# A hybrid decoder step on one Trainium2 core: the MLP and the gate by one level of Strassen's scheme

## The reference

```
def _channel_and_ple(h, mix, p_l, w_out, g_ffn, w_up, w_down, w_ple, w_ple_norm, w_ple_gate):
    h = h + mix @ w_out                                            # w_out 2048 x 2048
    u = _rmsnorm(h, g_ffn)
    h = h + jnp.square(jax.nn.relu(u @ w_up)) @ w_down             # 2048 x 8192, 8192 x 2048
    e = _rmsnorm(p_l @ w_ple, w_ple_norm) * jax.nn.sigmoid(h @ w_ple_gate)   # 256 x 2048, 2048 x 2048
    return h + e
```

## Time and profile before

| | |
|---|---|
| time, three runs | 2848.83, 2850.85, 2850.91 us; median 2850.85 |
| span of the profiled execution | 2847.1 us |
| PE busy over the span | 95% |
| DVE, ACT, POOL busy over the span | 46%, 27%, 20% |
| moved from HBM, written | 377.71 MB, 15.58 MB |

### The profile page before, as it was taken

The page is one execution under the profiler, slowest core; times in us unless marked ns, Lnnn a source line. Parts: engine busy times, 40 slices in busy tenths (PEclk is TensorE's granted clock), DMA queues, the critical chain, the costliest instruction groups (busy, mean ns, idle before and its releaser), DMA issues.

```text
span 2847.1 us, 50247 instructions
## 1 busy us (share of the span) xinstructions
PE 2696.2 (95%) x21759; PEld 2573.3 (90%) x21759; DVE 1320.5 (46%) x1501; ACT 774.8 (27%) x967; POOL 582.7 (20%) x290
## 2 busy tenths in 40 slices
PE   7999999967767999999999999999999999999998
PEld 7999999923346999999999999999999999999998
DVE  4277877628468224333333433333333333346433
ACT  3111111137643223222222222222222222223222
POOL 0098999300036011100000000000000000002322
PEclk9999999988876999999999999999999999999999
DMA  4388888489813222332333233333333333322233
GB/s 132 107 277 269 279 299 285 138 344 353 311 55 121 86 76 81 104 100 94 97 103 98 90 104 97 98 96 104 102 99 97 96 98 98 103 90 89 90 97 112
DMA packets 294896, 396.43 MB, mean 139 GB/s; under 512 B 14773, under 2 KB 256051, under 8 KB 292982
## 3 DMA queue, kind: packets, MB, share of 16 engines
q1 hardware_dynamic: 271688, 380.23, 40.4%
q10 hardware_dynamic: 22990, 13.01, 1.6%
HBM read 377.71 MB, written 15.58 MB: 138 GB/s over the span
## 4 chain that ended last, share of the span: by engine, by line
PE 79%; DVE 6%; POOL 5%; DMA 4%; issue 2%; SPq 2%; ACT 2%; ACTq 0%; DVEq 0%; POOLq 0%
PE ps L1180 25%; PE ps L1182 25%; PE ps L1185 25%; POOL kpage L1029 4%; DMA kpage<-in_cache_k 2%; DMA vpage<-in_cache_v 2%; DVE wl L1672 1%; PE ps L1280 1%; PE ps L1560 1%; SPq L470 1%; POOL dl L1074 1%; DMA xs<-in_x_sample 0%; ACT wh L608 0%; DVE se L1829 0%; POOL bx L1082 0%
## 5 line engine op out<-in xcount | busy, mean ns | idle before, releaser
L1180 PE MATMUL ps<-uh,wh 128*128 128x260 f32 x4512 | 1184.9, 284 | 20.1 <-DVE wl L1672 14.1
L1182 PE MATMUL ps<-ul,wh 128*128 128x260 f32 x4512 | 1180.5, 283 | 0.0
L1672 DVE TENSOR_TENSOR wl<-raw,wh 128x1024 fp32r<-128x1024 f32 (+1 forms) x418 | 590.4, 1413 | 1242.9 <-ACT wh L608 1242.8
L608 ACT ACTIVATE wh<-raw 128x1024 fp32r<-128x1024 f32 (+1 forms) x418 | 440.6, 1055 | 1803.6 <-PE ps L1185 1755.3
L1185 PE MATMUL ps<-uh,wl 128*128 128x260 f32 x4512 | 907.6, 283 | 0.0
L1180 PEld LDWEIGHTS ps<-uh,wh 128*128 128x128 f32 x4512 | 853.1, 189 | 22.9 <-DVE wl L1672 11.8
L1182 PEld LDWEIGHTS ps<-ul,wh 128*128 128x128 f32 x4512 | 851.3, 189 | 0.0
L1185 PEld LDWEIGHTS ps<-uh,wl 128*128 128x128 f32 x4512 | 696.4, 189 | 0.0
L1180 PE MATMUL ps<-hh,wh 128*128 128x260 f32 x2048 | 536.1, 283 | 0.0
L1182 PE MATMUL ps<-hl,wh 128*128 128x260 f32 x2048 | 534.1, 282 | 0.0
L1185 PE MATMUL ps<-hh,wl 128*128 128x260 f32 x2048 | 410.7, 282 | 0.0
(11 more groups left out here) (340 smaller groups left out, 1502.6 us busy)
## 6 DMA issues: line engine op xcount, KB each, us to landing
kpage<-in_cache_k SPq DMA_DIRECT2D x128, 512.0 KB, 4.9
vpage<-in_cache_v SPq DMA_DIRECT2D x128, 512.0 KB, 6.1
raw<-in_w_up SPq DMA_DIRECT2D x128, 512.0 KB, 3.6
raw<-in_w_down SPq DMA_DIRECT2D x128, 512.0 KB, 3.4
raw<-in_w_in SPq DMA_DIRECT2D x88, 512.0 KB, 4.6
raw<-in_w_out SPq DMA_DIRECT2D x32, 512.0 KB, 3.5
raw<-in_w_ple_gate SPq DMA_DIRECT2D x32, 512.0 KB, 3.4
xt<-in_x_prompt SPq DMA_DIRECT2D x8, 1024.0 KB, 9.0
```

The costliest lines, as they stand in the source:

```text
L608: A(wh[:, c % 2, 0:elems], raw[:, c % 2, 0:elems], ACT.Copy).then_inc(hi_ready, 1)
L1180: mm(ps[:, bank + 2 * m + f, 0:HALF], h_, xh[:, f * HALF:(f + 1) * HALF], start=st, stop=False)
L1182: mm(ps[:, bank + 2 * m + f, 0:HALF], h_, xl[:, f * HALF:(f + 1) * HALF], start=False, stop=False)
L1672: tt(wl[:, c % 2, 0:elems], raw[:, c % 2, 0:elems], wh[:, c % 2, 0:elems].bitcast(F32), ALU.subtract).then_inc(lo_ready, 1)
```

## The change

Up, down and gate each are products of a weight matrix with 520 token columns. They are now done by one level of Strassen's scheme (in Winograd's form). The weights are cut in even and odd tiles of 128 rows and of 128 columns, the activations in even and odd tiles of rows and in two halves of 260 tokens. A **group** is 2048 weight rows by 256 columns, as four blocks (11, 12, 21, 22) of 8 tiles each. A group takes 7 products instead of 8; each product is 8 tiles by 260 tokens in 24 matrix instructions (16 with the weights' high part, 8 with the rest). There are 72 groups: 32 of up (g 0 to 31), 32 of down (g 32 to 63, four chunks of 2048 hidden rows by 8 column groups), 8 of gate (g 64 to 71).

- DVE makes four sums of weight blocks for each group (`sum_t1` to `sum_t4`) and the rest of seven block operands (`w_low`). ACT makes the seven high parts (`w_high`).
- Seven operands of activations (`ah`, `al`, places 0 to 8) serve a whole phase: all of up, one chunk of down, or all of gate. A change of phase, from up to down, between chunks of down and from down to gate, is called a turning here. For down the operands' sums are made on POOL (`hidden_sums`) and stored in DRAM (`o_scr`) after each up group, and loaded back as 7 operands of 1040 KB (`operand`) at the turnings. There their second halves' rests are POOL's, from the third operand on (`a_low_second`), the others DVE's (`a_low`).
- The results of a group are combined from four PSUM banks by ACT and DVE in pieces of 128 x 260 (`x_rd`, `ev`). Up's pieces go through relu and square on ACT. The norm's factor is squared and applied only once, to the finished sum of down, on POOL (`h_complete`).
- Down's partial results lie in DRAM (`d_scr`); in chunks 1 to 3 they are loaded, added to (`add_first`, `add_second` on POOL, the rest on DVE) and stored again.
- PLE stands ahead of up, and h and e are kept in DRAM (`h_scr`, `e_scr`).
- Weight blocks have 128 columns, so rows of 512 bytes.

```diff
+GU, GD, GG = 0, 32, 64
+GN = 72
+KP = 8
+
+
+        def w_block(g, odd_rows, odd_cols):
+
+            if g < GD:
+                w, row, col = d["w_up"][0], 0, 256 * g
+            elif g < GG:
+                w, row, col = d["w_down"][0], 2048 * ((g - GD) // 8), 256 * ((g - GD) % 8)
+            else:
+                w, row, col = d["w_ple_gate"][0], 0, 256 * (g - GG)
+            w = w[row:row + 2048].rearrange("(j e p) n -> e p j n", e=2, p=P)
+            return w[odd_rows][:, :, col + P * odd_cols:col + P * odd_cols + P]
+
...
+                    load_out(SL_OUT + 4 * g + j)
+                h_store(g - 1)
...
-            for i in range((CHUNKS - 2) // 2):
-                load_up(SL_MLP + 8, 1, 2, 32, i)
-                load_down(SL_MLP + 16, 0, 2, 32, i)
-                load_up(SL_MLP + 24, 2, 2, 32, i)
-                load_down(SL_MLP + 32, 1, 2, 32, i)
...
+                if g == 1:
+                    h_store(7)
+                    for m in range(2):
+                        sp.wait_ge(h_out[m], 16 * 4)
+                    sp.wait_ge(s_hg, KT)
+                    block22(0)
+                    block12(0)
+                    block11(0)
+                    block22(1)
+                if g >= 3:
+                    e_store(g - 3)
+            e_store(5)
+            e_store(6)
+            sp.wait_ge(lo_ready, SL_ALL + 2)
+            block21(0)
+            e_store(7)
+
...
+            for g in range(GN):
+                if GD + 8 <= g + 1 < GG:
+                    down_load(g + 1)
+                if g > GD and g <= GG - 8:
+                    down_store(g - 1)
+                last_up, c = g == GD - 1, (g - GD) // 8
+                turning = last_up or (g >= GD and g < GG - 8 and (g - GD) % 8 == 7)
+                if turning:
+                    operand(c + 1, 2)
+                if g + 1 < GN:
+                    block12(g + 1)
+                if 1 <= g <= GD:
+                    hidden_store(g - 1)
+                if turning:
+                    operand(c + 1, 3)
+                    operand(c + 1, 4)
+                if g + 1 < GN:
+                    block11(g + 1)
+                if turning:
+                    operand(c + 1, 5)
+                if g + 1 < GN:
+                    block21(g + 1)
+                if turning:
+                    operand(c + 1, 6)
+                if g + 2 < GN:
+                    block22(g + 2)
+                if g == 27 or (g >= GD and g < GG - 8 and (g - GD) % 8 == 3):
+                    operand(c + 1, 0)
+                    operand(c + 1, 1)
...
+            def w_high(w):
+                g, i = w // 7, w % 7
+                if w < 2:
+                    act.wait_ge(w_used, SL_PLE + 6 + w + 3)
+                else:
+                    act.wait_ge(wh_used, WH_USED0 + w - 1)
+                    act.wait_ge(w_lo, W_LO0 + w - 1)
+                if i == 0:
+                    act.wait_ge(b_in[b11(g)], B_IN0[b11(g)] + 16 * (g + 1))
...
+                A(wh3[:, w % 2], w_source(g, i), ACT.Copy).then_inc(w_hi, 1)
...
+            def relu_square(g, k, src):
+                chain(A(st[:, k], src, ACT.Relu))
+                A(st[:, k], st[:, k], ACT.Square).then_inc(o_sq, 1)
...
+                        if up:
+                            if g:
+                                act.wait_ge(o_out, 16 * g)
+                            else:
+                                act.wait_ge(w_used, SL_ALL + 2)
+                            chain(A(st[:, 0], bank(g, 0), ACT.Relu))
+                            act.sem_inc(a_free, 1)
+                            A(st[:, 0], st[:, 0], ACT.Square).then_inc(o_sq, 1)
...
+            def hidden_sums(g):
+                pool.wait_ge(o_sq, O_SQ0 + 4 * g + 3)
+                step(pool.tensor_tensor(st[:, 4], st[:, 7], st[:, 5], ALU.add))
+                step(pool.tensor_tensor(st[:, 3], st[:, 0], st[:, 7], ALU.subtract))
+                step(pool.tensor_tensor(st[:, 1], st[:, 4], st[:, 0], ALU.subtract))
+                pool.wait_ge(o_sq, O_SQ0 + 4 * g + 4)
+                pool.tensor_tensor(st[:, 6], st[:, 2], st[:, 1], ALU.subtract).then_inc(o_sum, 1)
+
...
+            def add_first(g):
+                q = g - GD
+                both = dt3[q % 3].rearrange("p m n -> p (m n)")[:, HALF:3 * HALF].rearrange("p (x n) -> p x n", x=2)
+                pool.wait_ge(d_in[q % 3], D_IN0[q % 3] + 16 * ((q - 8) // 3 + 1))
+                pool.wait_ge(ev, EV0 + 5 * g + 1)
+                pool.tensor_tensor(both, both, xsc[:, 1].unsqueeze(1).to_broadcast([P, 2, HALF]), ALU.add)\
+                    .then_inc(d_add, 1)
+
+            def add_second(g):
+                part = dt3[(g - GD) % 3][:, 1, HALF:T]
+                pool.wait_ge(ev, EV0 + 5 * g + 2)
+                pool.tensor_tensor(part, part, xsc[:, 2], ALU.add).then_inc(d_add, 1)
+
+            def a_low_second(phase, i):
+                n = place_of(phase, i)
+                pool.wait_ge(a_hi, A_HI0 + 2 * (7 * phase + i) + 2)
+                pool.tensor_tensor(al[n][:, 4:8], af[n][:, 4:8], ah[n][:, 4:8].bitcast(F32), ALU.subtract)\
+                    .then_inc(al_p, 1)
+
...
+            def h_complete(g):
+                dt_ = dt3[(g - GD) % 3]
+                pool.wait_ge(ev, EV0 + 5 * g + 5)
+                if g == GG - 8:
+                    pool.wait_ge(r_sq, R_SQ0 + 1)
+                    pool.wait_ge(hr_in, 32)
+                step(pool.tensor_tensor(dt_, dt_, rstd.unsqueeze(1).to_broadcast([P, 2, T]), ALU.mult))
+                h_ = hT[:, g - GG + 8]
+                pool.tensor_tensor(h_, h_, dt_, ALU.add).then_inc(h_fin, 1)
...
+            BANK_OF = (0, 1, 0, 2, 3, 2, 3)
+
+            def product(g, i, phase):
+                w, n = 7 * g + i, place_of(phase, i)
+                pe.wait_ge(w_hi, W_HI0 + w + 1)
+                out, fresh = bank(g, BANK_OF[i]), i in (0, 1, 3, 4)
+                for k in range(KP):
+                    if g == GG and k == 7:
+                        pe.wait_ge(q_lo7, Q_LO70 + (0, 1, 2, 4, 5, 3, 6)[i] + 1)
+                    mm(out, wh3[:, w % 2, k], ah[n][:, k], start=fresh and k == 0, stop=False,
+                       skip_group_check=True)
+                    last = mm(out, wh3[:, w % 2, k], al[n][:, k], start=False, stop=False,
+                       skip_group_check=True)
+                last.then_inc(wh_used, 1)
+                pe.wait_ge(w_lo, W_LO0 + w + 1)
+                for k in range(KP):
+                    last = mm(out, wl3[:, w % 2, k], ah[n][:, k], start=False, stop=k == KP - 1,
+                              skip_group_check=True)
+                last.then_inc(wl_used, 1)
...
+            for g in range(GN):
+                c, j = (g - GD) // 8, (g - GD) % 8
+                phase = 0 if g < GD else min(1 + c, 4)
...
+                for i in range(7):
+                    if g == GU:
+                        pe.wait_ge(al_a, AL_A0 + i + 1)
+                        pe.wait_ge(al_b, AL_B0 + i + 1)
+                    elif GD <= g < GG and j == 0:
+                        pe.wait_ge(al_a, AL_A0 + 7 * phase + i + 1)
...
+                    if i == 5:
+                        pe.wait_ge(ev, EV0 + 5 * g + 2)
...
+            def sum_t3(g):
+                dve.wait_ge(b_in[b22(g)], B_IN0[b22(g)] + 16 * (g // 2 + 1))
+                dve.wait_ge(b_in[b12(g)], B_IN0[b12(g)] + 16 * (g + 1))
+                if g:
+                    dve.wait_ge(t_sum, T_SUM0 + 4 * (g - 1) + 3)
+                    dve.wait_ge(w_lo, W_LO0 + 7 * (g - 1) + 4)
+                tt(rb[B_T], rb[b22(g)], rb[b12(g)], ALU.subtract).then_inc(t_sum, 1)
+
+            def sum_t1(g):
+                dve.wait_ge(b_in[b11(g)], B_IN0[b11(g)] + 16 * (g + 1))
+                dve.wait_ge(t_sum, T_SUM0 + 4 * g + 1)
+                tt(rb[b12(g)], rb[b12(g)], rb[b11(g)], ALU.subtract).then_inc(t_sum, 1)
+
+            def sum_t2(g):
+                dve.wait_ge(t_sum, T_SUM0 + 4 * g + 2)
+                dve.wait_ge(w_lo, W_LO0 + 7 * g + 1)
+                tt(rb[b11(g)], rb[b11(g)], rb[B_T], ALU.add).then_inc(t_sum, 1)
+
+            def sum_t4(g):
+                dve.wait_ge(t_sum, T_SUM0 + 4 * g + 3)
+                dve.wait_ge(w_lo, W_LO0 + 7 * g + 3)
+                tt(rb[B21], rb[B21], rb[b11(g)], ALU.subtract).then_inc(t_sum, 1)
+
+            def w_low(w):
+                dve.wait_ge(w_hi, W_HI0 + w + 1)
+                if w >= 2:
+                    dve.wait_ge(wl_used, WL_USED0 + w - 1)
+                tt(wl3[:, w % 2], w_source(w // 7, w % 7), wh3[:, w % 2].bitcast(F32), ALU.subtract).then_inc(w_lo, 1)
+
...
+            def gate_pair7():
+                dt_ = dt3[(GG - 1 - GD) % 3]
+                dve.wait_ge(ev, EV0 + 5 * (GG - 1) + 5)
+                dve.wait_ge(hr_in, 32)
+                link(tt(dt_, dt_, rstd.unsqueeze(1).to_broadcast([P, 2, T]), ALU.mult))
+                tt(hT[:, 7], hT[:, 7], dt_, ALU.add).then_inc(h_fin, 1)
...
+                    if i == 6:
```

(29 more changed lines are left out.)

909 lines of the change are left out of this document (595 added, 314 removed).

## The result

The changed kernel takes **3015.38 us** (median of 4 runs, 3009.14 to 3019.8) against 2850.88 us (2848.83 to 2852.13) for the kernel before: a ratio of 1.0579, 95% interval 1.0562 to 1.0596. It is 5.8% slower where 4.3% faster was forecast. The profiled run has a span of 3007.4 us, 160.3 more than before.

What follows compares the result with a forecast made beforehand. PE's instruction list was taken to bound MLP and gate: -209.9 us, plus 29, 4, 21, 3, 8 and 21 of waits, gives -123.9 against the span of 2847.1, hence 2723.2 and a median of 2727 us; range 2680 to 2790.

Steps and rivals of the forecast that it cites:

- What bounds, PE's spacing, PE's list: MLP and gate: PE's instruction list bounds, 0.1198 us each; 13824 instructions become 12096, -209.9 us.
- Hidden with 1 us to spare: 0: Transfers in a group: hidden store lands near 11.5, product 5's high part ready at 13.5, due at 14.4; adds 0.
- rival 2: Hidden store lands 2 or 3 us later, costing 1 or 2 us in each of 31 groups: 2758 to 2789; chance 0.12.
- State updates: +4: Up groups with a state update: POOL's extra 5.7 us covered on average over three groups; 8 x 0.5, +4 us.
- Turnings +21: Four phase changes: DVE's and POOL's added work exceeds PE's time; 4.5 us three times, 8 from up to down, +21.
- Covered on average: State updates in up: three groups' DVE and POOL work is 55.8 us of PE's 60.3.
- Last chunk +3: Last chunk of down: `h_complete` adds 2.44 + 1.92 us to seven groups; +3 us, at most 10.
- Start of the gate +21: Groups 63 and 64: PE waits for gate operands; group 64 takes 42 us instead of 20.1, +21, at least 11.
- Gate groups +8: Gate groups: multiplication by e, scaling and additions on DVE and POOL cost seven times about 1.1, +8 us, at most 14.
- PLE and group 0 +29: PLE and up's first group: late w_ple, operands and rests; up starts in effect at T+59 instead of 29.8, +29 us.
- Rival 3: POOL's work is added in full to DVE's, no overlap: +46 us, 2773 us; chance 0.17.
- Rivals 1 and 4: 1: DVE's and POOL's sums hide, 2667 us, chance 0.18. 4: 512-byte-row blocks land late at `sum_t3`, slower than before, 0.04.

Runs made afterwards that it cites:

- store_first: Changed kernel with SyncE issuing the store of the hidden rows ahead of block 12 of the next group instead of behind it; 2886.67 us, ratio 1.0143.
- repeats: Changed kernel with ScalarE's piece behind product 5's high part, plus that high part made 4 to 16 times more in six down groups; 2986.84 us.
- no_state: Changed kernel with ScalarE's piece behind product 5's high part, minus GpSimd's three instructions of each state update in up; 2918.84 us.
- no_pool_mlp: `all1` with all of GpSimd's work in up and down moved to VectorE; 2793.1 us.
- all1: `store_first` plus state updates over three groups, gate's U3 ahead of third sum, gate's operands on VectorE, h completed behind the additions; 2859.96 us, ratio 1.0044.
- no_pool_all: `no_pool_mlp` with the gate's sums of squares and multiplication of e also moved from GpSimd to VectorE; 2780.67 us, ratio 0.9762.
- no_pool_late: `no_pool_all` with the store of the hidden rows behind block 12 again, as in the changed kernel; 2935.73 us.

## Why the prediction was wrong

**What bounds, PE's spacing, PE's list: right.** 20.1 us a group wherever nothing waits (third window of the result), -209.9 us.

**"Hidden with 1 us to spare: 0": the step that failed.** It is rival 2's mechanism at more than its size. The order of the store alone is worth 129 us, of 288 between forecast and measurement, 114 of them in groups 1 to 30: 3.8 us a group where rival 2's worst case had 2. Two numbers were off, both the same way. SyncE starts block 12 8.4 us into the group and not 5.6 (7.9 in `store_first`, in a group without any wait): `sum_t4` is queued behind product 2's rest, and that waits for its high part. In down the 5.6 was right: there SyncE starts it 5.8 us into group 34, which begins at 2077.9.

```profile
2083.69 0.37 SPq L657 DMA_DIRECT2D rb<-in_w_down  x1
```

In up ScalarE has relu and square of the last piece of the group before ahead of that high part in its queue, and 5.6 us leaves no room for them: the high part comes 4.2 us into group 13 of `store_first` and 2.1 us into group 34. The store lands 7.6 us after its issue and not 5.5: I added 1.4 us for the block in front, and `store_first` shows 3.0. Even from its own figures the sum was optimistic. How 3.2 us for 512 KB and 75% more bytes make the landing near 11.5 is not said; in proportion the store takes 5.6 us, which with the start at 5.6 and the 1.4 makes a landing at 12.6 and a high part at 14.6, behind the 14.4 at which it is due. 8.8 + 7.6 is 16.4, plus 2.0 for relu, square and high part is 18.4 against a due time of 14.4; the trace has 3.5 us of wait, as product 5 would have begun at 14.9 and not at 14.4. An estimate with 1 us of slack over a chain of five terms was booked at nothing and given 0.12, which the working does not bear out.

**The missing term: the clock.** The sum priced a wait at its own length. The trace has 72 us of starts at 1.2 GHz behind waits, 40 of them in up; `repeats` shows the wait to be the cause. The windows of the kernel before had shown the clock below 1 only outside the stretches that I priced, and nothing in the working asked what a wait does to it.

**"State updates: +4": too small.** The 3.2 us and their clock come to about 6 us in each of 8 groups (47 in `store_first`); `no_state` takes 25 off. "Covered on average" was the error: PE asks for each product's parts in turn, with 1 or 2 us of slack, and the three instructions come together.

**Turnings +21: 63.** They are 24.0 in groups 31 and 32, where the store takes part, and 12.9, 13.4 and 13.0. Both lists were added, which was right, but GpSimd's rest of 1040 was taken at 1.92 us: it takes 2.43 with VectorE idle and up to 3.45 beside it, three in a row 10.11. The lower clock (14 us of the 63) was left out. With all of the work on VectorE (`no_pool_mlp`) the turnings in down still cost 8.5 to 8.8 each, so the sharing explains only about a third; what holds the rest no run separates.

**Last chunk +3: 27.7.** 10 of it is group 57, where POOL stands 16.9 us for hT from DRAM ahead of the additions, which I did not cost at all, and 6 group 63. Groups 58 to 62 have a wait of up to 1.5 us each, from GpSimd's completion of h; when VectorE does it, groups 59 to 62 take 20.2.

**Start of the gate +21: 39.4.** The list was walked in the right order, with about 2.8 us for each of GpSimd's six instructions; they took 4.0 to 5.9 and made VectorE's as long.

**Gate groups +8: 31.9.** Where the wait was to be I had not said. It is mostly U3's (19.2 us), behind a third sum that waits 1.65 us for its block and then takes 3.08 beside GpSimd's 2.40.

**PLE and group 0 +29: 34.5.** Nearly right: the second group started at T+84, predicted T+79. GpSimd's instructions of 2080 elements took 5.4 and 5.5 us, where 3.1 were put in, and VectorE's two rests beside them 11.2.

**The rule on SBUF.** The Trainium skill, "SBUF — State Buffer", "Who interferes with whom", has the second of the two blocked until the first finishes. The traces agree in every pair shown here: VectorE's rest of 1820 elements, 2.04 us without GpSimd, took 5.87 when it began 1.05 us after a GpSimd instruction of 5.01. Rival 3 took it as "POOL's work is added in full", +46 on top of the part that the forecast already held. In the runs taking the work off GpSimd is worth 79 us (`all1` to `no_pool_all`), with the operands of the gate 96. When both engines had a queue they alternated, and both lists, not one, grew to the sum.

**Rivals 1 and 4.** Nothing hid (1). Blocks with 512-byte rows did land late, 4.8 us by the median in up (3.6 was taken, a median of the stm tiles' loads and stores together), and VectorE waited 37.9 us for them at `sum_t3`. In up this stayed hidden; in the gate groups it is 1.65 us of the delay of U3. So 4's outcome, slower than before, came almost without its mechanism, and for a cause that the forecast had priced at nothing. The chances were built as if the terms were independent small sizes; all of them lean on the same slack of 1 to 2 us.

**What stays open.** Why waits of the same length, anywhere from 2.7 to 3.9 us, are followed by the lower clock in some groups and not in others. Group 64 is still at 43.8 us and the turnings at 49 to 51 (40.3); a queue order that mends these was not tried.

## What to carry to other kernels

Before a change takes away TensorE's work, list for each queue the waits that stand ahead of what TensorE asks for next; a wait for a DRAM store on an engine that feeds TensorE needs its landing time from the trace, with what SyncE issues just before it, and a slack of 1 us over several estimated terms is not to be booked as nothing. VectorE and GpSimd were not two engines here: while both have two-input work on SBUF, count the sum on each, and try the whole work on the faster one. And price a wait of TensorE at more than itself: here waits of 2.7 us and more cost up to 2.7 us again at the lower clock.

## What the runs showed of the hardware

- The same 910 KB store landed in 7.6 us with a 512 KB load issued 0.4 us before it on the same queue, and in 4.6 us without.
- Inserted waits of TensorE of 1.9 and 3.0 us left the clock at 1.00; 4.1 us brought starts of 0.217 us, 1.6 us in all, and 15.0 us no more than 2.4 (`repeats`). Elsewhere waits of 2.7 and 2.9 us cost 1.6 too (`no_pool_late`), and two of 3.4 and 3.6 us 0.1 (groups 27 and 23 of the changed kernel).
- An instruction of 1820 elements with two inputs took GpSimd 4.01 to 5.87 us beside VectorE's work, and VectorE 2.04 to 2.60. 473.5 us of GpSimd's busy time, moved to VectorE, lengthened VectorE's by 6.2 us.
